# Two VectorE transposes and their DMA round trips, moved across an iteration boundary of a token mixer

## The chip, the cores and the metric

The kernel runs on one core of one Trainium2 chip. The metric is device time in microseconds (us), the median over the runs of a kernel. The engines named here are TensorE (PE: matrix products), VectorE (DVE: element-wise work and transposes of 32x32 blocks), ScalarE (ACT), GpSimd (POOL) and SyncE (SP), which here issues nearly all transfers between HBM and the on-chip SBUF. They run in parallel, each in its own program order, and are ordered against each other by semaphores alone.

## The reference

Two decoder layers over 256 tokens of width 1024. In each layer a token mixer runs dilated window attention (8 heads, 3 groups of keys) and chunkwise retention (4 heads of value width 512) from one input projection; then come gates, an output projection, a layer norm, and a gated convolutional MLP with its own layer norm. Cut to what the change touches:

```python
pr = jnp.exp(scores - m)
out = jnp.einsum('brhnqk,brhnkd->brhnqd', pr, vc) / denom     # attention: probabilities times values
...
y = (y - mu) * lax.rsqrt(var + GN_EPS)                        # retention: group norm of each head
y = y.reshape(b, s, h * dv) * g + bias
ret = silu(ret_g) * ret
merged = sigmoid(gate_a) * (attn @ w_attn_proj) + sigmoid(gate_r) * (ret @ w_ret_proj)
```

Both the probabilities and the normalised retention output are computed with tokens on the partitions and are needed the other way round: keys on the partitions for the product with the values, features on the partitions for the next projection.

## The kernel before

All weights stream from HBM in chunks of 1 MB through a ring of three slots. Each chunk is split in two so that float32 products keep their precision: ScalarE writes the high part (`to_hi`, L462), VectorE subtracts it from the raw chunk to get the low part (`to_lo`, L819, "the subtraction"), and TensorE multiplies with both. Slot reuse makes a circle: SP loads chunk c when VectorE has subtracted chunk c-3 (`load`, L287 to L294), ScalarE copies it when TensorE is done with chunk c-3, VectorE subtracts it, TensorE uses it.

The mixer of a layer is written out as four iterations (`mixer(l, j)`, j = 0 to 3) of 15 chunks each, c = 0 to 14; an iteration makes two attention heads and one retention head. After the fourth, a merge stage follows with chunks of its own, numbered from `C_MERGE`. So each layer has three boundaries between one iteration and the next ("inner turns", six in all) and one from the last iteration to the merge ("merge turns", two in all).

In iteration j, at c = 14, VectorE handles the second head (a = 1) of the pair and the retention head: mask and maximum, group statistics, the subtraction of the next iteration's chunk 1, then `normalise(1)` (L1024), `turn_prob(1)` (L1030: a transpose of 128x1024 values within 32x32 blocks), the two normalising writes of `ret_y` (L1103, L1105; they wait for POOL's reciprocal root, L1354), `turn_ret()` (L1035, a transpose of the same size), and `high_part(14)` (L976). The next iteration begins with the subtraction of chunk 2. TensorE's order there is: chunk 0 (values by token), then chunks 1 and 2 as one pair (L1380 to L1382, behind `weights_ready(g, c + 1)`, so behind the subtraction of chunk 2), then `attend(it)` (L1525, L1529: probabilities times values, first head 0, then head 1, each behind its `probT_in[a]`), then chunk 3.

A transpose of 32x32 blocks is only half of a transpose. The blocks are put in place by a round trip through HBM on SP's queue: `prob_out`/`ret_out` write 512 KB out (L310, one DMA), and, when that has landed, `prob_in`/`ret_in` read it back with the blocks exchanged (L316, four DMAs of 128 KB). What waits for them: TensorE's `attend` for the probabilities, ScalarE's `finish_ret` (L485) for the retention output. `finish_ret` alternates between ScalarE and VectorE and ends with `ret_lo` (L952). In the merge, TensorE's order is: two gate chunks, half of the retention projection, `attend`, then a wait for `ret_lo`, then the other half (L1394).

SP runs in program order as well. `turned_blocks(it, c)` (L335) is called from the list of loads after load c: behind load 4 it does, in this order, `prob_out(1)`, `ret_out`, `prob_in(1)`, `ret_in`; only then is load 5 issued.

Of the kernel before, what the change touches and what calls it, by code (L numbers as in the profile page):

```python
# [50 lines left out]
NJ = 4  # L51
# [46 lines left out]
def program(nc, x, xT, positions, w_in, w_attn_proj, w_ret_proj, w_out, w_up, w_down,  # L98
# [5 lines left out]
    with ctx:  # L104
# [3 lines left out]
        def sem(name):  # L108
            return ctx.enter_context(nc.semaphore(name))
# [20 lines left out]
        def view(start, shape):  # L130
# [22 lines left out]
        prob_flat = [view(a * TT * 512, (TT * 512,)) for a in range(2)]  # L153
        prob = view(2048, (TT, 512))
        decayed = view(3456, (384,))
        ret_y = view(3840, (TT, RV))
        ret_y_flat = view(3840, (TT * RV,))
# [6 lines left out]
        ret_t_flat = view(6912, (4 * SEQ,))  # L164
# [62 lines left out]
        exp_done, inv_ready, prob_ready = sem("exp_done"), sem("inv_ready"), sem("prob_ready")  # L227
        prob_turned, pv_done = sem("prob_turned"), sem("pv_done")
        prob_written = [sem(f"prob_written{a}") for a in range(2)]
        probT_in = [sem(f"probT_in{a}") for a in range(2)]  # L230
        ret_turned, ret_written, ret_yT_in = sem("ret_turned"), sem("ret_written"), sem("ret_yT_in")
# [6 lines left out]
        gn_stats, gn_mean_var, gn_var_eps, gn_rstd, ret_y_ready = (sem(n) for n in (  # L238
            "gn_stats", "gn_mean_var", "gn_var_eps", "gn_rstd", "ret_y_ready"))
# [17 lines left out]
        def bank_of(c):  # L257

            return {0: 0, 1: 2, 2: 1, 11: 2, 12: 3}[c]
# [15 lines left out]
        def slot(l, c):  # L275

            return (c + l * C_LAYER) % RING
# [8 lines left out]
        def _(sp):  # L286
            def load(l, g, c, src, width=CE):  # L287
                s = slot(l, c)
                dst = raw[:, s, 0:width]
                if len(src.shape) == 3:  # L290
                    dst = dst.rearrange("p (k n) -> p k n", k=src.shape[1])

                sp.wait_ge(lo_ready, g + c + 1)
                sp.dma_start(dst, src).then_inc(raw_loaded[s], 16)  # L294

            def part(w, l, k0, nk, n0, n):

                v = w.rearrange("l (k p) n -> l p k n", p=P)
                return v[l:l + 1, :, bass.ds(k0, nk), bass.ds(n0, n)].rearrange("l p k n -> (l p) k n")
# [27 lines left out]
            def ret_out(it):  # L327
                sp.wait_ge(ret_turned, it + 1)
                blocks_out(ret_blocks[:, :, :], ret_t_flat, ret_written)

            def ret_in(it):
                sp.wait_ge(ret_written, 16 * (it + 1))
                blocks_in(ret_y_flat, ret_blocks[:, :, :], ret_yT_in)

            def turned_blocks(it, c):  # L335

                if c == 1:
                    prob_out(0, it)
                if c == 2:
                    prob_in(0, it)  # L340
                if c == 4:
                    prob_out(1, it)
                    ret_out(it)
                    prob_in(1, it)
                    ret_in(it)

            def mixer_loads(l, j, c_from):
                rv, v0, v12, g01 = VALUES
# [19 lines left out]
            for l in range(DEPTH):  # L368
# [30 lines left out]
                turned_blocks(l * NJ + NJ - 1, 2)  # L399
                load(l, g, 3, part(w_ret_proj, l, KT, KT, 0, CH))  # L400
                load(l, g, 4, part(w_attn_proj, l, 0, KT, 0, CH))
                turned_blocks(l * NJ + NJ - 1, 4)
                for j in range(NJ - 2):
                    g = L0 + C_MERGE + j * 6
                    load(l, g, 5, part(w_in, l, 0, KT, j * CH + GA0 + CH, CH))
                    load(l, g, 6, part(w_out, l, j * 2, 2, 0, D))
                    load(l, g, 7, part(w_in, l, 0, KT, j * CH + GR0 + CH, CH))
                    load(l, g, 8, part(w_ret_proj, l, 0, KT, j * CH + CH, CH))
                    load(l, g, 9, part(w_ret_proj, l, KT, KT, j * CH + CH, CH))
                    load(l, g, 10, part(w_attn_proj, l, 0, KT, j * CH + CH, CH))  # L410
# [400 lines left out]
        def _(dve):  # L811
# [3 lines left out]
            def to_lo(l, g, c):  # L815

                dve.wait_ge(hi_ready, g + c + 1)
                s = slot(l, c)
                nc.vector.tensor_tensor(w_lo[:, s, :], raw[:, s, :], w_hi[:, s, :].bitcast(F32),  # L819
                                        ALU.subtract).then_inc(lo_ready, 1)  # L820
# [135 lines left out]
            def finish_attn(j, done):  # L956

                for a in range(2):
# [3 lines left out]
                                            attn_hi[:, j * 2 + a, :].bitcast(F32).rearrange("p (m r) -> p r m", r=2),  # L962
                                            ALU.subtract).then_inc(attn_lo_ready, 1)

            def mixer(l, j):
                it = l * NJ + j
                it2 = it * 2
# [56 lines left out]
                        ins = nc.vector.tensor_scalar(prob[:, t, :], prob[:, t, :], row_inv[:, t:t + 1], None, ALU.mult)  # L1024
                    ins.then_inc(prob_ready, 1)

                def turn_prob(a):

                    dve.wait_ge(prob_ready, it2 + a + 1)
                    nc.vector.transpose(prob_flat[a], prob.rearrange("p t k -> p (t k)")).then_inc(prob_turned, 1)  # L1030

                def turn_ret():

                    dve.wait_ge(ret_y_ready, it + 1)
                    nc.vector.transpose(ret_t_flat, ret_y_flat).then_inc(ret_turned, 1)  # L1035

                def decay_scores():
                    dve.wait_ge(ret_scores_done, it + 1)
                    nc.vector.tensor_tensor(decayed[:, 0:256], acc[3][:, 0:256], decay[:, j, :], ALU.mult)
# [19 lines left out]
                for c in range(C_MIX):  # L1059
                    if c == 14:  # L1060
                        high_part(13, silu[:, 0:2, :], 1.0)
                        mask_and_max(1)
                        group_stats()
                    if j or c:
                        to_lo(l, g, c + 2)
                    if j and c == 3:
                        finish_attn(j - 1, it)
                    if c in (rv, rv + 1):
                        t = c - rv
                        dve.wait_ge(rv_hi_ready, it2 + t + 1)  # L1070
                        if one_by_one:
                            nc.vector.tensor_tensor(rv_lo[:, :, t * CH:(t + 1) * CH],
                                                    bank[bank_of(c)][:, :].rearrange("p (t n) -> p t n", t=TT),
                                                    rv_hi[:, :, t * CH:(t + 1) * CH].bitcast(F32), ALU.subtract)\
                              .then_inc(bank_read[bank_of(c)], 1)
                        else:
                            nc.vector.tensor_tensor(rv_lo[:, t, :], bank[bank_of(c)][:, :], rv_hi[:, t, :].bitcast(F32),
                                                    ALU.subtract).then_inc(bank_read[bank_of(c)], 1)
                    if j and c == 1:
                        finish_ret(j - 1, it)  # L1080
                    if one_by_one and c == 3:
                        angle_turns()
                    if one_by_one and c == 4:
                        angle_remainders()
                    if c in (5, 6):
                        near_low(c - 5)
                    if c in range(3, 9):
                        high_part(c, qk[:, c - 3, :, :], ATT_SCALE if c % 2 == 1 else 1.0)
                    if c == 9:
                        rotate(0)  # L1090
                    if c == 10:
                        mask_and_max(0)
                        rotate(1)
                    if c == 11:
                        normalise(0)
                        turn_prob(0)
                    if c == 12:
                        decay_scores()
                    if c == 14:
                        normalise(1)  # L1100
                        turn_prob(1)
                        dve.wait_ge(gn_rstd, it + 1)
                        nc.vector.tensor_scalar(ret_y[:, 0, :], acc[2][:, :], mv_gn[:, 0, 0:1], rs_gn[:, 0:1],  # L1103
                                                ALU.subtract, ALU.mult)
                        nc.vector.tensor_scalar(ret_y[:, 1, :], acc[3][:, :], mv_gn[:, 1, 0:1], rs_gn[:, 1:2],  # L1105
                                                ALU.subtract, ALU.mult).then_inc(ret_y_ready, 1)
                        turn_ret()
                        high_part(14, silu[:, 2:4, :], 1.0)

            for l in range(DEPTH):  # L1110
# [7 lines left out]
                def low_sum(dst, j, u, k):  # L1118

                    dve.wait_ge(merge_low, l * (4 * NJ - 1) + 4 * j + k + 1)  # L1120
                    nc.vector.tensor_tensor(dst[:, u, :, :], pair[u][:, :, 0:SEQ], dst[:, u, :, :], ALU.add)\
                      .then_inc(bank_read[2 * u], 1)
# [28 lines left out]
                for c in range(5):  # L1151
                    to_lo(l, L0, c0 + c + 2)
                    if c == 0:
                        low_sum(gate_sum, 0, 0, 0)
                    if c == 1:
                        low_sum(gate_sum, 0, 1, 1)
                        finish_ret(NJ - 1, (l + 1) * NJ)
                    if c == 3:
                        finish_attn(NJ - 1, (l + 1) * NJ)
                        low_sum(prod_sum, 0, 0, 2)  # L1160
# [14 lines left out]
                j = NJ - 1  # L1175
# [659 lines left out]
```

## Time and profile before

| | us |
|---|---|
| median of 3 runs | 1491.69 |
| lowest, highest | 1491.23, 1495.32 |
| the profiled execution | 1495.06 |
| its span, first to last instruction | 1493.3 |
| PE busy | 1460.3 (98%) |
| DVE busy | 1047.4 (70%) |
| ACT busy | 768.7 (51%) |
| POOL busy | 45.9 (3%) |
| bytes moved | 292.00 MB, mean 196 GB/s |
| mean granted TensorE clock | 0.993 of full |

The profiled execution is one execution, 3.4 us above the median. "Busy" is the time in which an engine had an instruction in work; the idle time of an engine is put down to the engine and line whose semaphore ended it. The granted clock is the share of TensorE's full clock that the chip let through in a stretch. A line number is a line of the kernel before.

### The profile page before, as it was taken

Reading aid. Unit: us, or ns where it says so; the run is one execution under the profiler, and the core shown is the slowest. Engines: PE = TensorE matmul, PEld = TensorE weight load, DVE = VectorE, ACT = ScalarE, POOL = GpSimd, SP = SyncE. Lnnn points to the kernel's source line nnn. Section 1 sums busy time; section 2 is a strip of 40 time slices with the busy share of each in tenths; the row PEclk is TensorE's granted clock in tenths of the full one; section 3 lists DMA queues with packets and bytes.
Section 4 is the critical chain, followed back from the end, with each engine's and each line's share of the span. In section 5 each row is a group of like instructions: output and inputs, shape, how many; then the busy total and the mean of one; then the engine's idle time right before and its main releaser. Section 6 shows DMA issues by size and latency. Waiting matters only on the chain.

```text
span 1493.3 us, 20079 instructions
## 1 busy us (share of the span) xinstructions
PE 1460.3 (98%) x8177; PEld 1278.8 (86%) x8177; DVE 1047.4 (70%) x1189; ACT 768.7 (51%) x813; POOL 45.9 (3%) x30
## 2 busy tenths in 40 slices
PE   9999999999999999999999999999999999999998
PEld 8888888888888888888888888888887888888886
DVE  5775675857665588777857667667567556887777
ACT  5545454454554456566544454545545444566562
POOL 0000000000000020000000000000000000200000
PEclk9999999999999999999999999999999999999999
DMA  9777596685856564655555956857748664665571
GB/s 309 237 189 207 172 212 202 182 214 169 224 178 224 179 219 166 211 197 198 178 174 170 226 182 176 218 182 198 211 159 208 201 222 162 220 205 189 172 239 39
DMA packets 357420, 292.00 MB, mean 196 GB/s; under 512 B 104544, under 2 KB 347744, under 8 KB 356704
## 3 DMA queue, kind: packets, MB, share of 16 engines
q1 hardware_dynamic: 356528, 290.14, 64.4%
q8 instruction: 56, 0.92, 0.3%
q10 hardware_dynamic: 816, 0.79, 0.2%
q14 instruction: 20, 0.16, 0.0%
HBM read 277.27 MB, written 13.63 MB: 195 GB/s over the span
## 4 chain that ended last, share of the span: by engine, by line
PE 80%; DVE 11%; ACT 3%; DMA 3%; SPq 1%; issue 1%; DVEq 0%; ACTq 0%
PE bank L1394 34%; PE bank L1399 17%; PE bank L1380 6%; PE bank L1381 6%; PE bank L1382 6%; DVE w_lo L819 5%; PE acc L1380 3%; PE acc L1381 3%; PE acc L1382 3%; ACT w_hi L462 2%; DMA raw<-w_in 1%; SPq L316 1%; PE acc L1529 1%; DVE scratch L1030 1%; DVE stat L1015 1%
## 5 line engine op out<-in xcount | busy, mean ns | idle before, releaser
L819 DVE TENSOR_TENSOR w_lo<-raw,w_hi 128x2048 fp32r<-128x2048 f32 x234 | 535.4, 2289 | 201.7 <-ACT w_hi L462 201.3
L1394 PE MATMUL bank<-xT_both,w_hi 128*128 128x512 f32 x2208 | 528.4, 392 | 2.2 <-DVE scratch L976 2.2
L462 ACT ACTIVATE w_hi<-raw 128x2048 fp32r<-128x2048 f32 x241 | 459.3, 1908 | 118.6 <-PE bank L1382 50.8
L1394 PEld LDWEIGHTS bank<-xT_both,w_hi 128*128 128x128 f32 x2208 | 407.7, 188 | 83.5 <-DVE scratch L976 2.8
L1399 PEld LDWEIGHTS bank<-xT_both,w_lo 128*128 128x128 f32 x2208 | 283.1, 191 | 10.7
L1399 PE MATMUL bank<-xT_both,w_lo 128*128 128x256 f32 x2208 | 286.5, 283 | 0.0
L1380 PE MATMUL bank<-w_hi,xT_both 128*128 128x512 f32 (+1 forms) x464 | 164.2, 354 | 16.3 <-DVE w_lo L819 15.9
L1381 PE MATMUL bank<-w_lo,xT_both 128*128 128x512 f32 (+1 forms) x464 | 163.2, 352 | 0.0
L1382 PE MATMUL bank<-w_hi,xT_both 128*128 128x512 f32 (+1 forms) x464 | 162.8, 351 | 0.0
L573 ACT ACTIVATE scratch<-bank 128x512 f32<-128x512 f32 x80 | 47.6, 595 | 212.0 <-PE bank L1399 212.0
L1380 PEld LDWEIGHTS bank<-w_hi,xT_both 128*128 128x128 f32 x464 | 89.7, 193 | 29.2 <-issue 17.8
L1242 DVE SCALAR_TENSOR_TENSOR scratch<-scratch,feat 128x256 f32<-128x256 f32 x176 | 77.4, 481 | 33.7 <-ACT scratch L729 28.8
L1382 PEld LDWEIGHTS bank<-w_hi,xT_both 128*128 128x128 f32 x464 | 90.0, 194 | 11.2
L1381 PEld LDWEIGHTS bank<-w_lo,xT_both 128*128 128x128 f32 x464 | 89.9, 194 | 10.6
L976 DVE SCALAR_TENSOR_TENSOR scratch<-bank,scratch 128x512 f32<-128x512 f32 x80 | 54.8, 686 | 55.4 <-ACT scratch L573 55.3
L1380 PE MATMUL acc<-w_hi,mid_hi 128*128 128x512 f32 x224 | 87.8, 392 | 0.3 <-DVE mid_lo L838 0.3
L1381 PE MATMUL acc<-w_lo,mid_hi 128*128 128x512 f32 x224 | 87.6, 391 | 0.0
L1382 PE MATMUL acc<-w_hi,mid_lo 128*128 128x512 f32 x224 | 87.2, 389 | 0.0
L1394 PE MATMUL bank<-ret,w_hi 128*128 128x512 f32 x256 | 64.5, 407 | 5.2 <-DVE ret L952 5.2
L722 ACT ACTIVATE scratch<-bank 128x512 f32<-128x512 f32 x42 | 25.0, 596 | 86.0 <-PE bank L1399 86.0
L1394 PEld LDWEIGHTS bank<-ret,w_hi 128*128 128x128 f32 x256 | 49.4, 197 | 15.5 <-DVE ret L952 5.5
L1380 PEld LDWEIGHTS acc<-w_hi,mid_hi 128*128 128x128 f32 x224 | 42.2, 188 | 9.2 <-DVE mid_lo L838 1.2
(170 smaller groups left out, 1351.7 us busy)
## 6 DMA issues: line engine op xcount, KB each, us to landing
raw<-w_in SPq DMA_DIRECT2D x133, 1024.0 KB, 5.1
raw<-w_up SPq DMA_DIRECT2D x44, 1024.0 KB, 5.1
raw<-w_down SPq DMA_DIRECT2D x20, 1024.0 KB, 5.1
raw<-w_ret_proj SPq DMA_DIRECT2D x16, 1024.0 KB, 5.4
prob_blocks<-scratch SPq DMA_DIRECT2D x16, 512.0 KB, 4.3
scratch<-prob_blocks SPq DMA_DIRECT2D x64, 128.0 KB, 4.2
raw<-w_attn_proj SPq DMA_DIRECT2D x8, 1024.0 KB, 5.3
raw<-w_out SPq DMA_DIRECT2D x8, 1024.0 KB, 5.2
```

The costliest lines, as they stand in the source:

```text
L316: sp.dma_start(dst[v, :].rearrange("p (b r) -> p b r", r=32), src[:, :, v].rearrange("b (i p) r -> p (b i) r", p=32)).then_inc(landed, 16)
L462: nc.scalar.activation(w_hi[:, s, :], raw[:, s, :], ACT.Copy).then_inc(hi_ready, 1)
L573: nc.scalar.activation(dst, pair[pair_of(c)][:, :, SEQ:2 * SEQ], ACT.Copy, scale=ATT_SCALE if c in (3, 5, 7) else 1.0).then_inc(mix_low, 1)
L722: nc.scalar.activation(hpad[:, 2 * half:2 * half + 2, 2:2 + SEQ], pair[half][:, :, SEQ:2 * SEQ], ACT.Copy).then_inc(up_low, 1)
L819: nc.vector.tensor_tensor(w_lo[:, s, :], raw[:, s, :], w_hi[:, s, :].bitcast(F32), ALU.subtract).then_inc(lo_ready, 1)
L976: nc.vector.scalar_tensor_tensor(out=dst, in0=pair[pair_of(c)][:, :, 0:SEQ], scalar=scale, in1=dst, op0=ALU.mult, op1=ALU.add).then_inc(ba ...
L1242: ins = nc.vector.scalar_tensor_tensor(out=conv[:, 2 * half + b, :], in0=hpad[:, 2 * half + b, tap:tap + SEQ], scalar=feat[:, l, bass.ds(i ...
L1380: mm(dst, st_hi, mv_hi, start=start, stop=False)
L1381: mm(dst, st_hi, mv_lo, start=False, stop=False)
L1382: return mm(dst, st_lo, mv_hi, start=False, stop=stop)
L1394: mm(pair[p][:, m, :], hi[:, o:o + P], src[:, k0 + k, :, :].rearrange("p a t -> p (a t)"), start=first and k == 0, stop=False)
L1399: ins = mm(pair[p][:, m, SEQ:2 * SEQ], lo[:, o:o + P], src[:, k0 + k, 0, :], start=False, stop=last and k == KT - 1)
```

## The change

The two transposes leave c = 14 of their iteration. They are issued in the next iteration (or the merge) behind its first subtraction, the retention's first. SP's four steps move from behind load 4 to behind load 5 of the following iteration (or the merge), and the retention goes ahead of the probabilities in both the writes and the reads. Nothing is added to or taken from the computation; `turn_prob` and `turn_ret` now take the iteration as an argument and wait for the same semaphore counts as before.

```diff
-                if c == 4:
+                if c == 5:
+                    ret_out(it)
                     prob_out(1, it)
-                    ret_out(it)
+                    ret_in(it)
                     prob_in(1, it)
-                    ret_in(it)
...
                 load(l, g, 4, part(w_attn_proj, l, 0, KT, 0, CH))
-                turned_blocks(l * NJ + NJ - 1, 4)
                 for j in range(NJ - 2):
                     g = L0 + C_MERGE + j * 6
                     load(l, g, 5, part(w_in, l, 0, KT, j * CH + GA0 + CH, CH))
+                    if j == 0:
+                        turned_blocks(l * NJ + NJ - 1, 5)
...
+            def turn_prob(a, it):
+                dve.wait_ge(prob_ready, 2 * it + a + 1)
+                nc.vector.transpose(prob_flat[a], prob.rearrange("p t k -> p (t k)")).then_inc(prob_turned, 1)
+
+            def turn_ret(it):
+                dve.wait_ge(ret_y_ready, it + 1)
+                nc.vector.transpose(ret_t_flat, ret_y_flat).then_inc(ret_turned, 1)
...
                     if j or c:
                         to_lo(l, g, c + 2)
+                    if j and c == 0:
+                        turn_ret(it - 1)
+                        turn_prob(1, it - 1)
...
                     if c == 14:
                         normalise(1)
-                        turn_prob(1)
                         dve.wait_ge(gn_rstd, it + 1)
...
-                        turn_ret()
                         high_part(14, silu[:, 2:4, :], 1.0)
...
                 for c in range(5):
                     to_lo(l, L0, c0 + c + 2)
                     if c == 0:
+                        turn_ret((l + 1) * NJ - 1)
+                        turn_prob(1, (l + 1) * NJ - 1)
                         low_sum(gate_sum, 0, 0, 0)
```

## Rows read from the trace of the kernel before

**Rows 1.** The page's first part: busy time, share, instructions.
```profile
PE 1460.3 (98%) x8177; PEld 1278.8 (86%) x8177; DVE 1047.4 (70%) x1189; ACT 768.7 (51%) x813; POOL 45.9 (3%) x30
```
**Rows 2.** Waits of PE: who for whom, total us, times, longest.
```profile
PE bank L1380 <- DVE w_lo L819: 15.9, 6, 2.7
PE bank L1394 <- DVE ret L952: 5.2, 2, 2.8
```
**Rows 3.** The chain of waits, inner turn at 203.56: start, us, what.
```profile
196.71 1.25 DVE scratch L1030
...
199.40 1.25 DVE scratch L1035
...
201.22 2.21 DVE w_lo L819
...
203.56 0.47 PE bank L1380
```
**Rows 4.** Timeline of PE, two inner turns: start, us; idle before in brackets.
```profile
203.56 0.47 PE L1380 MATMUL bank<-w_hi,xT_both 128*128 128x512 f32 x1 [2.64 <-DVE w_lo L819]
...
216.17 0.82 PE L1525 MATMUL acc<-scratch 128*128 128x256 f32 x4
...
217.72 0.82 PE L1525 MATMUL acc<-scratch 128*128 128x256 f32 x4
...
219.19 0.71 PE L1394 MATMUL bank<-xT_both,w_hi 128*128 128x512 f32 x2
...
301.40 0.47 PE L1380 MATMUL bank<-w_hi,xT_both 128*128 128x512 f32 x1 [2.65 <-DVE w_lo L819]
...
312.41 0.82 PE L1525 MATMUL acc<-scratch 128*128 128x256 f32 x4
```
**Rows 5.** Stretches of 4 us: PE busy, granted clock, DMA share, GB/s.
```profile
205.00:209.00 4.00, 4.00 (x12) 0.57 1.33 155
```
**Rows 6.** Timeline of SP's queue, the same inner turn: issue start, us.
```profile
195.70 0.39 SPq L294 DMA_DIRECT2D raw<-w_in  x1
197.98 0.37 SPq L310 DMA_DIRECT2D prob_blocks<-scratch  x1
200.67 0.37 SPq L310 DMA_DIRECT2D ret_blocks<-scratch  x1
202.26 2.67 SPq L316 DMA_DIRECT2D scratch<-prob_blocks  x4
```
**Rows 7.** Timeline of ACT and of POOL, the same turn.
```profile
212.07 2.08 ACT L485 ACTIVATE scratch<-scratch,feat 128x256 f32<-128x256 f32 x4 [0.55 <-DMA scratch<-ret_blocks]
...
193.56 2.75 POOL L1354 TENSOR_TENSOR stat<-stat 128x2 f32<-128x2 f32 x1 [93.48 <-DVE stat L1057]
```
**Rows 8.** DMA issues, whole span: count, KB each, median us to landing.
```profile
raw<-w_in SPq DMA_DIRECT2D x133, 1024.0 KB, 5.1
...
scratch<-prob_blocks SPq DMA_DIRECT2D x64, 128.0 KB, 4.2
...
ret_blocks<-scratch SPq DMA_DIRECT2D x8, 512.0 KB, 3.5
```
**Rows 9.** Timelines of PE, SP and ACT at the two merge turns.
```profile
395.35 3.93 PE L1394 MATMUL bank<-xT_both,w_hi 128*128 128x512 f32 x16 [0.55 <-DVE scratch L976]
...
396.77 2.45 SPq L316 DMA_DIRECT2D scratch<-prob_blocks  x4
...
406.44 2.08 ACT L485 ACTIVATE scratch<-scratch,feat 128x256 f32<-128x256 f32 x4 [4.62 <-DMA scratch<-ret_blocks]
...
412.18 5.55 PE L1394 MATMUL bank<-ret,w_hi 128*128 128x512 f32 x16 [2.32 <-DVE ret L952]
...
1137.22 3.42 SPq L316 DMA_DIRECT2D scratch<-prob_blocks  x4
...
1147.65 2.07 ACT L485 ACTIVATE scratch<-scratch,feat 128x256 f32<-128x256 f32 x4 [5.13 <-DMA scratch<-ret_blocks]
...
1153.38 5.50 PE L1394 MATMUL bank<-ret,w_hi 128*128 128x512 f32 x16 [2.84 <-DVE ret L952]
```

More of the change, by code:

```diff
@@ L1025, in normalise @@
                     ins.then_inc(prob_ready, 1)
[L1027 to L1035, printed above, removed]
                 def decay_scores():
@@ L1095, in mixer @@
                         normalise(0)
-                        turn_prob(0)
+                        turn_prob(0, it)
                     if c == 12:
```

## The prediction

> **What bounds the kernel now.** I read the page first: PE is busy for 1460.3 of 1493.3 us [rows 1], so a change can gain only where PE stands idle or at a low clock, and loses wherever it makes PE wait. The waits of PE come next. Two of them lie at the turns that the change touches [rows 2]: six times PE waits up to 2.7 us for a subtraction (15.9 us in all, the largest wait it has), twice up to 2.8 us for `ret_lo` (5.2 us). The chain of waits through one inner turn shows what stands before the subtraction [rows 3]: both transposes, 1.25 us each, lie on it back to back with the rest of VectorE's work, and PE goes on at 203.56. The timeline of PE gives the cost [rows 4]: 2.64 us idle, and then 12.61 us (203.56 to 216.17) for the pair of chunks 1 and 2, where the turn at 301.40 takes 11.01 us for the same work. The difference of 1.6 us is a stretch at a granted clock of 0.57 on average over 4 us [rows 5], the lower of the two levels (1.2 GHz) for most of it; before it PE had stood idle for 2.64 us. By the timeline three of the six inner turns have such a stretch and three have not, at the same idle time. At both merge turns the chunk behind the idle time takes 5.5 us [rows 9] against 3.65 us for this group of 16 elsewhere in the chain, 1.9 us more.
>
> The second thing is the round trip through HBM, which PE's `attend` and ScalarE's `finish_ret` need. SP's queue shows it in steps [rows 6]: a 1 MB load at 195.70, the probabilities' write 2.28 us behind it, landed by 202.26 when the reads begin; the last of the eight reads lands at 212.07, where ScalarE starts [rows 7]. So a write behind a load lands 6.56 us after the load's issue, and eight reads take 9.81 us from first issue to last landing (9.67 and 10.43 us at the merge turns [rows 9]). Before the change the probabilities are the first four reads, so they land some 6 us after 202.26, and `attend` at 216.17 never waits.
>
> **What is removed.** At an inner turn each transpose takes 1.24 us off the chain (start of the next instruction minus its own start), 2.48 us together. The reciprocal root from POOL is ready at 193.56 + 2.75 = 196.31 [rows 7], before VectorE now asks for it at 196.71, so it doesn't become late. The subtraction ends at 200.95 and PE resumes at 201.08, 0.16 us after it fell idle. Six turns: -14.9 us. With so little idle time the three low-clock stretches behind it should go as well: -3 x 1.6 = -4.8 us. At the merge turns the 0.55 us in front of the second gate chunk [rows 9] goes, but PE there ends up at another wait, below, so it counts for nothing.
>
> **What is moved, with its queue.** This part decides. In the turn at 203.56, in new times: load 5 needs the subtraction of chunk 2 and is issued at 200.98. It now stands ahead of the turned blocks; before, it came behind all their reads. `turn_ret` ends at 202.20, the retention's write is issued at 202.22; `turn_prob` ends at 203.44 and its write goes out at 203.46. Both queue behind 1 MB. From the row above, the first write behind a load lands 6.56 us after the load's issue: 207.54. SP waits for that, then issues the retention's four reads, then the probabilities' four; the second write lands 1.6 us or so behind the first, as before, in time. Eight reads: 207.54 + 9.8 = 217.3 for the last, and the last are now the probabilities. `attend` for head 0 doesn't wait (its blocks were turned at c = 11): it starts at 201.08 + 11.01 = 212.09 and ends, after 1.55 us [rows 4], at 213.64. Head 1 waits from there to 217.3: 3.7 us. Its products and the step to chunk 3 take 1.5 us, so chunk 3 starts at 218.8. Before, it started at 219.19 in this turn, 15.63 us behind 203.56, and 14.03 us behind it in a turn without the low clock (11.01 + 3.02). New it is 15.3 us in either: -0.35 us in three turns, +1.25 us in three, +2.7 us in sum. The gain of the first paragraph is contained in this.
>
> The new idle time of 3.7 us is longer than any of those shown, and half or more of those were followed by a low clock. Bounds: 3 stretches of 1.6 us (4.8 us) to 6 of 1.9 us (11.4 us), or none if the chip does not react. I take 5 of 1.9 us, +9.5 us: it falls on a chunk of the same kind as the one at 412.18, the nearest row.
>
> What else waits in these queues: behind ScalarE's wait for the retention blocks stand `finish_ret` and the copies of chunks 4 and 5. The retention's reads go first; with issues of 2.7 us for four [rows 6] and 4.2 us for the last to land [rows 8] they take 6.2 us and land at 213.7, 1.7 us later than now. From there `finish_ret` takes 5.7 us (406.44 to 412.18 in the merge), then a subtraction of 2.21 us and a short one: some 222.3, before chunk 4 needs them at 218.8 + 5.6 = 224.4. It costs nothing; without that margin it would cost what it is late. Load 6 is issued behind the reads, some 4.5 us later than now, and is needed only four chunks on: nothing. The transposes in their new place stand ahead of the subtraction of chunk 3, for which PE has 11 us: nothing.
>
> **The merge turns.** The subtraction there ends at 394.97 in new times (395.35, where PE now goes on behind the instruction before it, plus 2.1, minus 2.48), the retention's write lands at 394.97 + 6.56 = 401.5, its reads 6.2 us later at 407.7 instead of 406.44. From there to PE's product with `ret_lo` it is 5.74 us [rows 9]: 413.5 against 412.18, +1.3 us. In the second merge turn, 740.70 us later by its PE rows, the reads before landed late (1147.65), so the same sum gives +0.8 us. Head 1's products would be done by 401.5 + 9.8 + 1.5 = 412.8, just ahead of that. Low clock behind the idle time: as before in both. Together +2.1 us.
>
> **Sum.** +2.7 + 9.5 + 2.1 = +14.3 us on the profiled execution's 1495.06 us (span 1493.3). Taken to the median, 1491.69: 1506.0 us.
>
> **Rivals.**
> (a) The wait comes but no low clock follows it: +2.7 + 2.1 = +4.8 us, 1496.5. For it: three idle times of 2.65 us passed without. Against it: 3.7 us is more.
> (b) The other side, faster: the write doesn't stand behind load 5. The place is SP's queue. The shortest price for a write is 3.5 us from issue to landing [rows 8]; the retention's write then lands at 205.7, the last read at 215.5, head 1 waits 1.9 us and chunk 3 starts at 217.0: -2.2 us in three turns and -0.6 in three, -8.2; the merge turns -1.5; with two low-clock stretches left, +3.8. Sum -5.9, 1485.8 us. For it: the 3.5 us rows. Against it: these writes had half a megabyte in front, not one, and the load at 195.70 lands in the median 5.1 us of all loads [rows 6, 8], undisturbed by the write behind it, which is what a queue served in order looks like. It decides from where the round trip is 1.8 us (14.3 over 8 turns) shorter than in my sum.
> The Trainium skill bears on this rival (DMA: Bandwidth & Descriptors, section "Queues, rings and completion order"): on each of the 16 DMA engines descriptors are consumed in ring order, and the increment of the semaphore lands only after every earlier write of that engine. By that rule the write's completion can't come before the load's, and (b) would lose most of its gain; the rows on the load and the write behind it agree, though no row here shows a write 1.25 us behind a load.
> (c) The round trip is hidden whole, by reads that are much faster with nothing else in the queue: -14.9 - 4.8 and the merge's 0.5 twice, -20.7, 1471 us. It needs the reads to land 3.7 us earlier; against it, all the turns' reads took 9.6 us or more.
> (d) The two idle times simply exchange: within 0.3% of before, 1492.
>
> **Chances.** Forecast 0.63 (its own range 1499 to 1513), (a) 0.13, (b) 0.14, (c) 0.05, (d) 0.05. A measurement of this kernel can tell about 0.3%, 4.5 us. Slower: the forecast and half of (a), with what of (b) and (d) strays there, 0.70; same: the rest of (a), most of (d), 0.10; faster: (b) and (c) and a little, 0.20. Range 1486 to 1514: the lower end takes in (b), the upper has six full low-clock stretches and a round trip some 0.7 us longer.
>
> **What would show it.** In the changed kernel's trace: PE's wait for the subtraction at the inner turns down from 2.6 to under 0.3 us; a new wait of PE at L1529's or L1525's second group, ended by the DMA into the probabilities, of 3.7 us six times; four reads of the retention issued about 6.6 us behind load 5; granted clock below 1 after the new wait and not after the old place. Wrong would be: the write landing under 5 us after its issue (rival b), no wait at `attend` (c), or the wait for the subtraction still there because something else of VectorE's fills the time.

## The result, and the profile after

The changed kernel takes 1515.48 us, median of 4 runs (1513.29 to 1516.22), against 1493.51 us before, median of 4 (1491.23 to 1495.57): ratio 1.0145, 95% interval 1.0123 to 1.0167. In a second series it was 1.0132 (1.0115 to 1.0149; 1513.53 against 1494.93 us). It is slower, by 19 to 22 us, 4 to 8 us more than forecast. The profiled execution took 1513.29 us, 18.2 us more than the one before.

The page of the kernel after, its first and fourth part, answers to [rows 1]: the work is the same, PE's share is a point lower, and DMA now holds 7% of the chain that ended last, where it had 3% (the page of before, same line: PE 80%, DMA 3%).

```profile
span 1511.5 us, 20079 instructions
PE 1467.1 (97%) x8177; PEld 1284.9 (85%) x8177; DVE 1045.9 (69%) x1189; ACT 769.4 (51%) x813; POOL 45.9 (3%) x30
...
PE 75%; DVE 11%; DMA 7%; SPq 3%; ACT 3%; issue 1%; DVEq 0%; ACTq 0%
```

PE's waits of after, total, times, longest. Both entries of [rows 2] are gone: no wait for a subtraction is listed at the turns. In their place stands one wait for the reads of the probabilities at all eight.

```profile
PE acc L1529 <- DMA scratch<-prob_blocks: 32.7, 8, 4.5
...
PE bank L1398 <- DVE scratch L987: 0.9, 1, 0.9
```

The last line answers to this one of before:

```profile
PE bank L1394 <- DVE scratch L976: 2.2, 3, 1.1
```

The inner turn that answers to [rows 4], in PE's timeline of after (start, us, what, idle before it). From the pair of chunks at 204.36 to head 0 of `attend` are 10.97 us, without low clock. Head 1 waits 3.85 us; its products then take twice their usual time (1.65 against 0.82), and chunk 3 starts 19.54 us behind 204.36. Before, it started 15.63 us (with low clock) or 14.03 us behind the same product, but that product then stood behind 2.64 us of idle time, of which some 0.16 us are left.

```profile
204.36 0.47 PE L1384 MATMUL bank<-w_hi,xT_both 128*128 128x512 f32 x1
...
215.33 0.82 PE L1529 MATMUL acc<-scratch 128*128 128x256 f32 x4
...
220.89 1.65 PE L1529 MATMUL acc<-scratch 128*128 128x256 f32 x4 [3.85 <-DMA scratch<-prob_blocks]
...
223.90 4.06 PE L1398 MATMUL bank<-xT_both,w_hi 128*128 128x512 f32 x16
```

SP's queue of the same turn, issue start and us, against [rows 6]. Load 5, then the retention's write 1.16 us behind it, landed when the reads begin at 211.11: 6.87 us after the load's issue, 5.7 after its own. The last read lands 9.8 us later. Over all eight turns the write lands 6.9 to 7.6 us after load 5's issue, so the turn shown is the quickest.

```profile
204.24 0.37 SPq L294 DMA_DIRECT2D raw<-w_in  x1
205.40 0.37 SPq L310 DMA_DIRECT2D ret_blocks<-scratch  x1
206.52 0.37 SPq L310 DMA_DIRECT2D prob_blocks<-scratch  x1
211.11 2.73 SPq L316 DMA_DIRECT2D scratch<-ret_blocks  x4
214.24 2.80 SPq L316 DMA_DIRECT2D scratch<-prob_blocks  x4
```

The list of DMA issues of after has the retention's eight writes at a median of 5.9 us from issue to landing, where [rows 8] has 3.5:

```profile
ret_blocks<-scratch SPq DMA_DIRECT2D x8, 512.0 KB, 5.9
```

ScalarE there, answering to [rows 7]: the retention's blocks land 5.9 us after the first read.

```profile
216.98 2.07 ACT L486 ACTIVATE scratch<-scratch,feat 128x256 f32<-128x256 f32 x4 [6.30 <-DMA scratch<-ret_blocks]
```

The granted clock of after behind the new wait, in stretches of 4 us (PE busy, clock, DMA, GB/s), against 0.57 in [rows 5]. The third inner turn has two low stretches in a row, the first of which begins while PE still waits (320.00 to 320.50).

```profile
222.00:226.00 4.00, 4.00 (x20) 0.72 0.21 65
319.00:323.00 4.00, 2.44 (x9) 0.60 0.84 262
320.00:320.50 0.50, 0.00 (x0) 0.50 1.00 324
323.00:327.00 4.00, 4.00 (x14) 0.54 0.03 8
```

Wider windows over the turns count them. Over 10 us behind head 1 the clock is 0.83 at seven of the eight turns of after, which is 1.7 us lost at each, and 0.72 over 12 us at the third, twice as much: nine low stretches, seven at inner turns and two at merge turns. Before, it is 0.83 at three inner turns (203, 846, 944) and at both merge turns, and 1.00 at the other three: five.

```profile
117.00:127.00 10.00, 5.93 (x26) 0.83 0.77 141
316.00:328.00 12.00, 7.88 (x29) 0.72 0.60 148
```

The first merge turn of after, PE's timeline, against [rows 9]: head 1 of `attend` is now what waits, 4.34 us, and the product with `ret_lo` follows it without a wait.

```profile
415.36 0.81 PE L1529 MATMUL acc<-scratch 128*128 128x256 f32 x4
...
421.41 0.92 PE L1529 MATMUL acc<-scratch 128*128 128x256 f32 x4 [4.34 <-DMA scratch<-prob_blocks]
...
423.68 2.54 PE L1398 MATMUL bank<-ret,w_hi 128*128 128x512 f32 x6
```

The 18.2 us between the two profiled executions, accounted for: the waits of PE shown went from 15.9 + 5.2 + 2.2 = 23.3 to 32.7 + 0.9 = 33.6 us, +10.3 (1.1 of the 2.2 us, and the 0.9, lie at 36 us, ahead of all the turns), and about 0.16 us is left at each of six turns, +1.0. The mean granted clock went from 0.993 to 0.989: (1 - 0.989) x 1511.5 - (1 - 0.993) x 1493.3 = +6.2 us; four more low stretches of 1.7 us would be 6.8. Sum +17.5 us.

### The profile page after: what moved, and what is told of

It is laid out like the page before. It is cut to its first block, busy times and chain, and to the rows that moved or that the text cites. A ratio compares the mean times of both kernels' runs of the same rounds, so it can differ in the third digit from the quotient of the medians.

```text
span 1511.5 us, 20079 instructions
## 1 busy us (share of the span) xinstructions
PE 1467.1 (97%) x8177; PEld 1284.9 (85%) x8177; DVE 1045.9 (69%) x1189; ACT 769.4 (51%) x813; POOL 45.9 (3%) x30
## 4 chain that ended last, share of the span: by engine, by line
PE 75%; DVE 11%; DMA 7%; SPq 3%; ACT 3%; issue 1%; DVEq 0%; ACTq 0%
PE bank L1398 33%; PE bank L1403 17%; DVE w_lo L820 5%; PE bank L1384 4%; PE bank L1386 4%; PE bank L1385 4%; PE acc L1384 3%; PE acc L1385 3%; PE acc L1386 3%; DMA ret_blocks<-scratch 3%; SPq L316 3%; DMA scratch<-prob_blocks 2%; ACT w_hi L463 2%; DMA raw<-w_in 1%; PE acc L1533 1%
## 5 line engine op out<-in xcount | busy, mean ns | idle before, releaser
L1384 PE MATMUL bank<-w_hi,xT_both 128*128 128x512 f32 (+1 forms) x464 | 162.1, 349 | 1.2 <-DVE xT_both L888 0.3
L1386 PE MATMUL bank<-w_hi,xT_both 128*128 128x512 f32 (+1 forms) x464 | 161.0, 347 | 0.0
L951 DVE TENSOR_TENSOR scratch<-scratch 128x1024 f32<-128x1024 f32 x8 | 9.8, 1225 | 65.3 <-ACT scratch L486 65.3
```

The lines of the kernel that those rows point to most:

```text
L1384: mm(dst, st_hi, mv_hi, start=start, stop=False)
L1386: return mm(dst, st_lo, mv_hi, start=False, stop=stop)
```

## The experiments

Each ratio is to the kernel before on the same chip, from five rounds.

| kernel | median, us | ratio | 95% interval | clock of the profiled run |
|---|---|---|---|---|
| changed, again | 1513.53 | 1.0132 | 1.0115 to 1.0149 | 0.989 |
| changed, idle time filled | 1501.99 | 1.0044 | 1.0030 to 1.0059 | 0.999 |
| before, idle time filled | 1487.78 | 0.9950 | 0.9935 to 0.9966 | 0.998 |
| changed, SP behind load 4 | 1484.65 | 0.9926 | 0.9911 to 0.9941 | 0.997 |
| changed, probabilities first | 1537.86 | 1.0282 | 1.0267 to 1.0296 | 0.982 |
| SP's half alone | 1537.86 | 1.0288 | 1.0274 to 1.0302 | 0.980 |
| probabilities' transpose alone | 1480.41 | 0.9904 | 0.9888 to 0.9919 | 0.998 |
| the same, filled | 1478.89 | 0.9890 | 0.9875 to 0.9905 | 0.999 |
| retention's transpose alone | 1508.90 | 1.0100 | 1.0086 to 1.0113 | 0.989 |

**The low clock by itself, in the changed kernel.** PE gets work that nobody needs in the new idle time; the products go into a PSUM tile that head 1 then overwrites.

```diff
                 for a in range(2):
+                    if a == 1:
+                        for _ in range(16):
+                            mm(acc[1][:, :], xT_both[:, 1, 0, 0:P], xT_both[:, 0, :, :].rearrange("p a t -> p (a t)"),
+                               start=True, stop=True)
                     pe.wait_ge(probT_in[a], 64 * done)
```

> The changed kernel with 16 products of 128x512 put into the idle time before head 1 of attend (they write a PSUM tile that head 1 then overwrites; the output is the same). At 0.23 us each they take 3.7 us of a wait of 3.7 to 4.5 us, so they delay nothing. Theory (the low clock is a term of its own, caused by the new idle time, and counts about 1.7 us for each of nine stretches): 1500 to 1503 us, granted clock near 1, PE's waits for the probabilities down to under 1 us each. Rival (the low clock has another cause, or the excess over the prediction lies in later landings alone): no change, 1513 to 1517 us, clock 0.987.

Measured 1501.99 us, clock 0.999. PE's timeline of this kernel at the same inner turn: the 16 products fill most of the wait, 0.45 us are left, and head 1 runs at its usual speed.

```profile
214.85 3.91 PE L1526 MATMUL acc<-xT_both 128*128 128x512 f32 x16
219.21 0.92 PE L1533 MATMUL acc<-scratch 128*128 128x256 f32 x4 [0.45 <-DMA scratch<-prob_blocks]
```

Its waits, total, times, longest, 0.3 to 1.8 us each, where I had expected under 1 us:

```profile
PE acc L1533 <- DMA scratch<-prob_blocks: 5.5, 7, 1.8
```

Products and waits together are 8 x 3.65 + 5.5 = 34.7 us, 2 us more than the wait that they replace, and yet the kernel is 13 to 15 us faster (1.0132 or 1.0145 against 1.0044). So the low clock costs the changed kernel some 15 us or a little more, which is what nine stretches of 1.7 us make, and what remains over the kernel before, 0.44%, is idle time, set against a kernel before that has its own low clock.

**The same in the kernel before.**

```diff
+                    if j and c == rv:
+                        pe.wait_ge(scores_masked, it2)
+                        for _ in range(11):
+                            mm(acc[1][:, :], xT_both[:, 1, 0, 0:P], xT_both[:, 0, :, :].rearrange("p a t -> p (a t)"),
+                               start=True, stop=True)
                     bank_free(c)
                     if c in (rv, v12):
                         weights_ready(g, c + 1)
```

> The kernel before with 11 such products (2.5 us) ahead of the pair of chunks 1 and 2, in the 2.64 us in which PE waits for the subtraction, at the six inner turns only; the output is the same. Theory: the three low-clock stretches of the inner turns go, those of the two merge turns stay: about -5 us, 1488 us, ratio 0.9965. Rival: no change, because the idle time and not the clock costs.

Measured 1487.78 us, 0.5% faster, a little more than expected; clock 0.998 where the kernel before has 0.990 to 0.994 in its nine executions. One of the two low stretches that were expected to stay is gone as well in the profiled execution: behind the wait of 2.58 us at the first merge turn there is one, behind that of 1.50 us at the second there is none. The same idle time, filled, costs 7 us less.

**The changed kernel again.**

> The changed kernel once more, in five rounds, to have its low clock over more executions than one. If the low clock makes the difference to the filled kernel (ratio 1.0044), the five executions show a granted clock of 0.986 to 0.989 and a time that rises as it falls, about 1.5 us for each 0.001, ratio 1.012 to 1.016. If the excess over the forecast lies elsewhere, time and clock don't go together.

Measured, time and granted clock of four executions: 1511.63 (0.989), 1512.33 (0.989), 1514.73 (0.988), 1517.45 (0.986). With the four of the first series (1513.29 at 0.989 to 1516.22 at 0.986) time rises as the clock falls, about 1.4 us for 0.001, where 1.5 was expected. The trace of the first of them again has nine low stretches, one behind each of the eight waits (3.39 to 4.55 us) and the double one at the second inner turn instead of the third. The executions at 0.986 must have had more, two or three by the clock; none of them was profiled, so where these lie isn't shown. Both profiled executions are at 0.989, the high end.

**The megabyte ahead of the write.** SP's steps go back behind load 4; all else as in the change.

```diff
-                if c == 5:
+                if c == 4:
                     ret_out(it)
...
                 load(l, g, 4, part(w_attn_proj, l, 0, KT, 0, CH))
+                turned_blocks(l * NJ + NJ - 1, 4)
...
-                    if j == 0:
-                        turned_blocks(l * NJ + NJ - 1, 5)
```

> The changed kernel with SP's four steps back behind load 4, the retention still first; VectorE as in the changed kernel. Takes away the megabyte ahead of the writes. Theory (the write queues behind load 5): it lands about 3.5 us after its issue instead of 5.7, PE's wait for head 1 falls from 4 to about 1.9 us, most low-clock stretches go; about 8 us under the kernel before, 1485 us, ratio 0.995. Rival (load 5 is not in the way, the two steps of writing and reading alone take that long): within 3 us of the changed kernel, ratio 1.012 to 1.015.

Measured 1484.65 us, on the expectation, with two low stretches left in its trace. SP's queue of this kernel at the second inner turn: the write is issued at 200.86 and the reads begin at 204.17, 3.3 us, against 5.7 us behind load 5.

```profile
200.86 0.37 SPq L310 DMA_DIRECT2D ret_blocks<-scratch  x1
201.99 0.37 SPq L310 DMA_DIRECT2D prob_blocks<-scratch  x1
204.17 2.82 SPq L316 DMA_DIRECT2D scratch<-ret_blocks  x4
```

Its waits of PE: still eight at head 1, but 1.9 us each.

```profile
PE acc L1528 <- DMA scratch<-prob_blocks: 15.4, 8, 2.7
```

With the load out of the way, both transposes behind the subtraction are a gain of 0.7%; with the load in front they are a loss of 1.4%. That is 2% for the place of one load.

**SP's half alone.** VectorE keeps both transposes at c = 14 (the two calls back behind `normalise(1)` and behind `ret_y`, the new calls removed).

```diff
                         normalise(1)
+                        turn_prob(1, it)
...
+                        turn_ret(it)
...
-                        turn_ret(it - 1)
-                        turn_prob(1, it - 1)
```

> SP's half of the change alone: load 5 first, then retention, then probabilities; VectorE as before the change, both transposes at c = 14. Theory (the megabyte and the order of the reads make the loss, and VectorE's half gives back): the subtraction wait of 2.64 us stays, the write goes out behind load 5 at 203.5 in the times of the inner turn shown, the last read lands near 220, chunk 3 starts 2 to 4 us later than before at each inner turn, ret_lo 3.9 us later at the merge turns, and low clock follows both: about 1525 us, ratio 1.020 to 1.025. Rival (VectorE's half, the transposes ahead of chunk 3's subtraction, makes the loss): near the kernel before, ratio under 1.005.

Measured 1537.86 us, ratio 1.0288, more than expected. Its waits of PE: the old wait is untouched and the new one is there as well.

```profile
PE acc L1526 <- DMA scratch<-prob_blocks: 31.4, 8, 7.6
PE bank L1381 <- DVE w_lo L820: 15.9, 6, 2.7
```

So VectorE's half gave back 1.4 to 1.6 points of the 2.9 that SP's half costs; two sets of idle times had two sets of low clock (0.980). Within SP's half, the place behind load 5 and the order of the reads were not taken apart.

**The order within the round trip.** As the change, but the probabilities first in transposes, writes and reads.

```diff
-                    ret_out(it)
                     prob_out(1, it)
-                    ret_in(it)
+                    ret_out(it)
                     prob_in(1, it)
+                    ret_in(it)
...
-                        turn_ret(it - 1)
                         turn_prob(1, it - 1)
+                        turn_ret(it - 1)
```

> The changed kernel with the probabilities first: transpose, write and reads. Theory: PE's wait for head 1 nearly goes (3.6 us earlier), but the retention lands 3.6 us later, and chunk 4 then waits for the end of the chain through finish_ret about 5 us; at the merge turns ret_lo is 3.6 us later. About 1518 to 1522 us, a bit slower than the changed kernel. Rival (the probabilities are all that PE needs in time): faster than the changed kernel by 20 us or more, near 1493.

Measured 1537.86 us: the sign was right and the size, 1518 to 1522, too small. Waits of PE:

```profile
PE bank L1398 <- DVE mid_lo L1081: 36.5, 6, 7.0
PE bank L1398 <- DVE ret L953: 15.0, 2, 7.6
PE acc L1529 <- DMA scratch<-prob_blocks: 3.5, 4, 1.8
```

The wait moved from head 1 to chunk 4, through ScalarE's `finish_ret`, which stands in front of what chunk 4 needs. I had expected 5 us there, it was 6.1, and low clock behind all of it (0.982). In the changed kernel the same chain had room, as predicted: no such wait is listed.

**One transpose moved.** The first kernel moves the probabilities' alone, with SP behind load 4, retention first. The second moves the retention's alone, probabilities first; its SP does the probabilities' write and reads before it issues the retention's write. The diff of the first against the kernel before:

```diff
                 if c == 4:
-                    prob_out(1, it)
                     ret_out(it)
-                    prob_in(1, it)
+                    prob_out(1, it)
                     ret_in(it)
+                    prob_in(1, it)
...
                         to_lo(l, g, c + 2)
+                    if j and c == 0:
+                        turn_prob(1, it - 1)
...
                         normalise(1)
-                        turn_prob(1)
```

> Only the probabilities' transpose moves behind the first subtraction; the retention's stays at c = 14; SP stays behind load 4 with the retention first. Theory: the subtraction comes 1.24 us earlier (-7.4 us), the wait that is left is 1.4 us and little low clock follows (-5 to -8), the probabilities land near 213.2 in the times of the turn shown, before head 1 needs them at 214.9, and the retention lands 2 us earlier than before, which takes about 2 us off each merge turn (-4): 1473 to 1478 us, ratio 0.985 to 0.989, no wait of PE at attend. Rival (what pays is only the PE idle time, and the two writes and reads don't fit): as with SP behind load 4 and both moved, ratio 0.993, with a wait at attend of 1 us or more.

> The mirror image: only the retention's transpose moves, the probabilities' stays at c = 14 and their write and reads go first, SP behind load 4. Theory: no wait at attend, but the retention lands near 214.7 instead of 212.07 and the chain through finish_ret makes chunk 4 wait about 2 us, at the merge turns ret_lo is about 3 us later: the 1.24 us per turn are given back, ratio 0.998 to 1.006. Rival (finish_ret has room): as one_moved, 0.986.

Measured 1480.41 and 1508.90 us. Waits of PE in the first:

```profile
PE bank L1382 <- DVE w_lo L819: 8.4, 6, 1.4
PE acc L1527 <- DMA scratch<-prob_blocks: 4.0, 3, 2.5
```

and in the second, ratio 1.0100, above its expectation:

```profile
PE bank L1396 <- DVE mid_lo L1079: 14.1, 6, 3.5
PE bank L1396 <- DVE ret L952: 11.8, 2, 5.9
PE bank L1382 <- DVE w_lo L819: 8.4, 6, 1.4
```

Both take 1.25 us per turn off the wait for the subtraction (2.65 to 1.4). The first pays for it with 4 us at three turns, two of them the merge turns, where the wait for `ret_lo` goes from 5.2 to 0.2 us. It misses the upper end of its expectation by 2.4 us, less than those 4 us, which I had put at nothing. No low stretch follows any of its waits. The second pays with 14.1 us at chunk 4 and with 11.8 us for `ret_lo`, where it was 5.2: some 21 us more, and its clock falls to 0.989. I had expected 2 us at chunk 4 (it was 2.4 on average) and 3 us more at each merge turn (3.3), and had counted no more low clock. Part of this is the order on SP and not the transpose: in the second inner turn `turn_ret` ends at 204.93, but the retention's write is issued at 206.43, behind the four reads of the probabilities. The mirror image with the writes interleaved as in the first kernel was not run.

**The same, with 5 products (1.15 us) in the rest of the wait**, by the same lines as above.

> The same with 5 products of 128x512 (1.15 us) in what is left of the wait for the subtraction at the inner turns; the output is the same. If an idle time of 1.4 us brings no low clock, the same time as without them, within 0.3%; if it does at some turns, up to 5 us less.

Measured 1478.89 us; its interval and that of the kernel without them overlap, so no difference is shown. That fits the kernel without them, where no low stretch followed those waits. It is the fastest median of the study, 1.1% under the kernel before.

## Why the prediction was right and where it was wrong

The direction and the mechanism held. The wait for the subtraction went, and the new wait stands where it was put, at head 1 of `attend` at each of the six inner turns, ended by the reads of the probabilities. Retention landed in time for chunk 4. Rival (b), a write not held up by load 5, is refuted: it landed 6.87 us after the load's issue, and with the load moved away 3.3 us after its own. By the rule of the Trainium skill that was named with it (DMA: Bandwidth & Descriptors, section "Queues, rings and completion order") the write can't complete ahead of the load, and the trace agrees, now also for a write issued 1.16 us behind: load 5 lands 5.3 us after its issue at 204.24, so at 209.5, and the write at 211.1. Rivals (a), (c) and (d) fell with the clock of 0.989, the eight waits, and the size.

The size was wrong: 14.3 us forecast, 18.2 between the profiled executions, 19 to 22 between medians, with 1515.48 us just above the range's 1514. Some of that excess over the range is the start of the sum: it was taken to a median of 1491.69 us from three runs, and later medians of the kernel before were 1494.9 to 1495.2. From 1495 the sum gives 1509.3, and 1515.48 is still 6 us above it (1513.53, the median of the second series, 4 us). Two terms of the sum were mis-sized, the first by some 4 us and the second by some 2.

First, the low clock, "I take 5 of 1.9 us" less "3 x 1.6": +4.7 us. The profiled execution shows +6.2 us by its mean clock, with seven low stretches at the inner turns where I had put five, and over executions it is more: before runs at 0.993 or 0.994 in most, after at 0.986 to 0.989, so (1 - 0.9875) x 1515 - (1 - 0.9935) x 1495 = about +9 us. I had allowed at most one stretch for each inner turn; the third turn had two in a row, and I read the number of stretches off one execution of the kernel before, although by the granted clock it varies from one execution to the next. The cost of one was closer: 1.7 us, where I had 1.6 and 1.9. The filled kernels show that this term is real and apart from the idle time.

Second, the idle time: by the same sum (+2.7 with the 4.8 us of low clock taken out, and +2.1) it was +9.6 us, and it was +11.3. The wait at an inner turn was 3.75 to 4.34 us, on average 4.0, not 3.7, six times 0.3 us: the write behind load 5 took 6.9 to 7.6 us, on average 7.1, instead of 6.56, less 0.1 us by which the reads were quicker and 0.16 us by which head 0 ended later. (The sum was worked out with the idle time and the low clock of three turns in one term, so this splits it: 2.7 + 4.8 is the idle part.) At the merge turns "`ret_lo`" was named as what would be last. It was head 1 instead, with waits of 4.34 and 4.47 us. That too comes of the low clock, which stretched head 1's products at the first merge turn from 1.5 to 2.27 us: in the filled kernel, without low clock, `ret_lo` is last again, by 0.3 us.

In the two profiled executions seven of the nine low stretches lie at inner turns and two at merge turns. How they divide in the executions at 0.986 isn't shown. Why a wait is followed by one stretch or by two stays open.

## What to carry to other kernels

When a step is moved past an instruction on one engine, follow its transfers through the queue they share: here the transposes were worth moving, and the load that came to stand in front of their write turned a gain of 0.7% into a loss of 1.4%. When two results share a round trip, time both consumers: with both transposes moved and load 5 in front, either order made one of the two consumers wait (32.7 us at head 1, or 36.5 us at chunk 4), while moving only the probabilities', whose consumer had more room, gained 1% at a cost of 4 us of new waits. Count a new idle time of TensorE twice, once as idle and once as the low clock that may follow it, and take the number of low stretches from several executions, not from one.

## What the runs showed of the hardware

Products without a use, put into an idle time of 2.6 to 4.5 us, made both kernels faster: 0.5% before the change, about 0.9 to 1.0% after it. The mean granted clock of a kernel is not the same from run to run: 0.986 to 0.989 for the changed one, at 1517 to 1512 us. A stretch of low clock can begin while TensorE still waits: from 320.00 to 320.50, in a wait of 4.12 us, it is 0.50, and at 220.89 the first products behind the wait already ran at half speed, where before the change, at 203.56, the first six ran at full speed and the next eight at half. Which idle times were followed by the low level (1.2 GHz) differs: all sixteen waits of 3.39 to 4.55 us in the two traces of the changed kernel were; so were those of 2.32 and 2.84 us in the kernel before, and of its six of 2.65 us three were and three were not. A wait of 3.02 us in the kernel with only the retention's transpose moved was not, nor were, with only the probabilities' moved, one of 2.47 us and six of 1.40 us. So the length of the wait alone doesn't decide.
